# A two-block transformer kernel on one core: its SBUF tiles allocated from both ends, with other start addresses

## The reference, cut to what matters

```python
# first block, DEPTH = 2 layers
h = rms_norm(x, attn_norm_g[l])
pa, pb, pc = split_sizes(h @ w_in[l], (A_PROJ, B_PROJ, C_PROJ))
ya, yb, yc = rwkv7_mixer(pa, ...), dilated_mixer(pb, ...), mla_mixer(pc, ...)
x = x + jnp.concatenate([ya, yb, yc], axis=-1) @ w_out[l]
h = rms_norm(x, ffn_norm_g[l])
x = x + (jax.nn.silu(h @ ffn_w_gate[l]) * (h @ ffn_w_up[l])) @ ffn_w_down[l]   # D_FF = 2816
# second block, DEPTH = 2 layers
#   h @ w_in_2 (IN_COLS = 3584), stick-breaking, MoBA and memory attention, gates,
#   x = x + mixed @ w_out_2, then a last rms_norm
```

## The kernel before, in words

| tile | start | modulo 1024 | minus w_hi, modulo 1024 |
|---|---|---|---|
| w_hi (and w_lo, w_raw) | 58560 | 192 | 0 |
| act_hi, act_lo | 24704, 32896 | 128 | -64 |
| mixed_hi, mixed_lo | 106240, 114432 | 768 | -448 |
| gated_hi, gated_lo, layer 0 | 131328, 153856 | 256 | +64 |
| gated_hi, gated_lo, layer 1 | 131424, 153952 | 352 | +160 |
| mem_hi, mem_lo | 131424, 139616 | 352 | +160 |

## Time and profile before

### The profile page before, as it was taken

The page is one execution under the profiler, slowest core; times in us unless marked ns, Lnnn a source line. Parts: engine busy times, 40 slices in busy tenths (PEclk is TensorE's granted clock), DMA queues, the critical chain, the costliest instruction groups (busy, mean ns, idle before and its releaser), DMA issues.

```text
span 967.2 us, 20420 instructions
## 1 busy us (share of the span) xinstructions
PE 937.9 (97%) x8862; PEld 886.4 (92%) x8862; DVE 680.7 (70%) x972; ACT 554.6 (57%) x851; POOL 7.6 (1%) x12
## 2 busy tenths in 40 slices
PE   8899999999999999999999999999999999999996
PEld 7788799999999988878999999998899899999896
DVE  6898666866744679966776666348699677698674
ACT  6873466645443578355654444337487666486565
POOL 0000000000000001000000000000000000000000
PEclk9999999999999999999999999999999999999999
DMA  9341115565555433211466654554353335453241
GB/s 337 159 165 55 46 58 194 205 228 210 180 194 198 175 128 135 89 46 46 155 218 229 242 189 174 185 199 140 131 175 131 94 137 189 149 174 135 94 141 69
DMA packets 23145, 149.89 MB, mean 155 GB/s; under 512 B 2576, under 2 KB 2832, under 8 KB 6032
## 3 DMA queue, kind: packets, MB, share of 16 engines
q1 hardware_dynamic: 23056, 148.59, 43.2%
HBM read 147.26 MB, written 1.05 MB: 153 GB/s over the span
## 4 chain that ended last, share of the span: by engine, by line
PE 68%; DVE 18%; ACT 9%; issue 2%; DMA 1%; SPq 0%; DVEq 0%; ACTq 0%
PE bank L1889 8%; PE bank L1890 8%; PE bank L1891 8%; DVE w_lo L275 6%; PE bank L2109 4%; PE bank L1912 4%; PE bank L1911 4%; PE bank L1913 4%; ACT w_hi L269 3%; PE bank L2110 3%; PE bank L2111 3%; PE bank L2114 2%; PE bank L2116 2%; PE bank L2115 2%; ACT act_hi L372 1%
## 5 line engine op out<-in xcount | busy, mean ns | idle before, releaser
L275 DVE TENSOR_TENSOR w_lo<-w_raw,w_hi 128x1024 fp32r<-128x1024 f32 x256 | 306.4, 1225 | 108.5 <-ACT w_hi L269 107.6
L269 ACT ACTIVATE w_hi<-w_raw 128x1024 fp32r<-128x1024 f32 x256 | 259.5, 1053 | 209.0 <-PE bank L1891 103.3
L1889 PE MATMUL bank<-act_hi,w_hi 128*128 128x256 f32 x704 | 196.7, 279 | 1.6 <-DVE w_lo L275 1.0
L1890 PE MATMUL bank<-act_lo,w_hi 128*128 128x256 f32 x704 | 195.9, 278 | 0.0
L1891 PE MATMUL bank<-act_hi,w_lo 128*128 128x256 f32 x704 | 195.9, 278 | 0.0
L1889 PEld LDWEIGHTS bank<-act_hi,w_hi 128*128 128x128 f32 x704 | 133.5, 190 | 2.4 <-issue 1.4
L1890 PEld LDWEIGHTS bank<-act_lo,w_hi 128*128 128x128 f32 x704 | 132.2, 188 | 0.1
L1891 PEld LDWEIGHTS bank<-act_hi,w_lo 128*128 128x128 f32 x704 | 132.1, 188 | 0.0
L2109 PE MATMUL bank<-act_hi,w_hi 128*128 128x256 f32 x352 | 100.7, 286 | 3.9 <-DVE w_lo L275 2.4
L1912 PE MATMUL bank<-gated_lo,w_hi 128*128 128x256 f32 x352 | 98.7, 280 | 0.0
L1911 PE MATMUL bank<-gated_hi,w_hi 128*128 128x256 f32 x352 | 98.5, 280 | 0.0
(11 more groups left out here) (370 smaller groups left out, 1994.7 us busy)
## 6 DMA issues: line engine op xcount, KB each, us to landing
w_raw<-in_w_ffn SPq DMA_DIRECT2D x66, 1024.0 KB, 4.8
w_raw<-in_w_mix SPq DMA_DIRECT2D x62, 1024.0 KB, 4.9
small_w<-in_small SPq DMA_DIRECT2D x2, 1280.0 KB, 7.5
w_raw<-in_w_mix SPq DMA_DIRECT2D x8, 256.0 KB, 6.0
x_res<-in_x_channels SPq DMA_DIRECT2D x4, 256.0 KB, 5.6
probs<-in_w_mix SPq DMA_DIRECT2D x2, 512.0 KB, 7.5
probsT<-in_w_mix SPq DMA_DIRECT2D x1, 1024.0 KB, 10.2
mem<-in_mem_channels SPq DMA_DIRECT2D x1, 1024.0 KB, 7.4
```

The lines of the kernel that those rows point to most:

```text
L269: self.nc.scalar.activation(hi, self.piece(self.raw_slot(g), p), ACT.Copy).then_inc(self.hi_ready, 1)
L275: self.nc.vector.tensor_tensor(lo, self.piece(self.raw_slot(g), p), hi.bitcast(fp32), ALU.subtract).then_inc(self.lo_ready, 1)
L1889: TE.matmul(o, hi[:, w], HI[:, k, :], start=(k == 0 and x == 0), stop=False)
L1890: TE.matmul(o, hi[:, w], LO[:, k, :], start=False, stop=False)
```

## The change

Tiles can now be allocated from the upper end downwards (`top=True`). The weight stream's three tiles, the squares, norms, constants, parameters and tables go to the upper end; the activation pairs and the stages' own tiles stay at the lower end. Four unused tiles are added: `between` (128 bytes) above the weights, `below_mixed` (32 bytes), `below_gated` (96 bytes, in layer 1 alone) and `below_mem` (64 bytes). No instruction, size, order or semaphore is changed; only start addresses are.

```diff
+BETWEEN = 32
...
-        raw = K.sb("w_raw", [P, 2, CHUNK])
-        hi, lo = K.sb("w_hi", [P, 2, CHUNK], f32r), K.sb("w_lo", [P, 2, CHUNK], f32r)
+        raw = K.sb("w_raw", [P, 2, CHUNK], top=True)
+        hi, lo = (K.sb(f"w_{x}", [P, 2, CHUNK], f32r, top=True) for x in ("hi", "lo"))
...
-        self.PRMS = self.sb("prm", [P, WIDTH["prm"] + N_PRMS])
+        self.PRMS = self.sb("prm", [P, WIDTH["prm"] + N_PRMS], top=True)
+        self.RSALL = self.sb("norm_rs", [P, T + NT], top=True)
+        self.cst_sb = {"both": self.sb("consts_both", [P, WIDTH["both"]], top=True), "prm": self.PRMS}
+        self.sb("between", [P, BETWEEN], top=True)
         self.st = Stream(self)
...
-        return (c or self.ctx).enter_context(self.nc.sbuf_tensor(name, shape, dt))
+        return (c or self.ctx).enter_context(
+            self.nc.sbuf_tensor(name, shape, dt, side="right" if top else "left"))
...
+    if layer:
+        K.sb("below_gated", [P, 24], c=c)
     GHI = K.sb("gated_hi", [P, FK, T], f32r, c)
...
+    K.sb("below_mem", [P, 16], c=c)
     MHI = K.sb("mem_hi", [P, KT, T], f32r, c)
...
-            first["rope_tables"] = K.sb("rope_tables", [P, 4, T], c=c)
-            first["positions"] = K.sb("positions", [P, T], i32, c)[:, :]
+            K.sb("below_mixed", [P, 8], c=c)
+            first["rope_tables"] = K.sb("rope_tables", [P, 4, T], c=c, top=True)
+            first["positions"] = K.sb("positions", [P, T], i32, c=c, top=True)[:, :]
...
-            second["mem"] = K.sb("mem", [P, KT, T], c=c)[:, :, :]
-            second["gates"] = K.sb("gates", [P, 8, T], c=c)
+            second["mem"] = K.sb("mem", [P, KT, T], c=c, top=True)[:, :, :]
+            second["gates"] = K.sb("gates", [P, 8, T], c=c, top=True)
```

More of the change, by code:

```diff
@@ L302, in __init__, with sb @@
         self.LO = self.sb("act_lo", [P, KT, T], f32r)
-        self.PRMS = self.sb("prm", [P, WIDTH["prm"] + N_PRMS])
+        self.PRMS = self.sb("prm", [P, WIDTH["prm"] + N_PRMS], top=True)
+        self.RSALL = self.sb("norm_rs", [P, T + NT], top=True)
+        self.cst_sb = {"both": self.sb("consts_both", [P, WIDTH["both"]], top=True), "prm": self.PRMS}
+        self.sb("between", [P, BETWEEN], top=True)
         self.st = Stream(self)
-        self.SQ = self.sb("squares", [P, 3, 512])
-        self.RSALL = self.sb("norm_rs", [P, T + NT])
+        self.SQ = self.sb("squares", [P, 3, 512], top=True)
         self.RSB, self.RS = self.RSALL[:, 0:T], self.RSALL[:, T:T + NT]
-        self.cst_sb = {"both": self.sb("consts_both", [P, WIDTH["both"]]), "prm": self.PRMS}
         self.PS = ctx.enter_context(nc.psum_tensor("bank", [P, 8 * 512], fp32))
         self.banks = [self.PS[:, 512 * i:512 * (i + 1)] for i in range(8)]
-    def sb(self, name, shape, dt=fp32, c=None):
+    def sb(self, name, shape, dt=fp32, c=None, top=False):
         self.named[name] = self.named.get(name, -1) + 1
         name = f"{name}_{self.named[name]}" if c else name
-        return (c or self.ctx).enter_context(self.nc.sbuf_tensor(name, shape, dt))
+        return (c or self.ctx).enter_context(
+            self.nc.sbuf_tensor(name, shape, dt, side="right" if top else "left"))
     def sem(self, name):
@@ L2789, in program @@
         K = Kernel(nc, ctx, io)
-        GAINS = K.sb("gains", [P, KT])
+        GAINS = K.sb("gains", [P, KT], top=True)
         block = ctx.enter_context(nc.Block())
@@ L2800, in program @@
             K.sb("small_w_end", [P, N_SMALL + 4 * T - 2 * KT * T], c=c)
-            K.cst_sb["first"] = K.sb("consts_first", [P, WIDTH["first"]], c=c)
+            K.cst_sb["first"] = K.sb("consts_first", [P, WIDTH["first"]], c=c, top=True)
             stage_start(K, block, norm, GAINS[:, :], first)
@@ L2815, in program @@
         with ExitStack() as c:
-            K.cst_sb["second"] = K.sb("consts_second", [P, WIDTH["second"]], c=c)
-            second["mem"] = K.sb("mem", [P, KT, T], c=c)[:, :, :]
-            second["gates"] = K.sb("gates", [P, 8, T], c=c)
+            K.cst_sb["second"] = K.sb("consts_second", [P, WIDTH["second"]], c=c, top=True)
+            second["mem"] = K.sb("mem", [P, KT, T], c=c, top=True)[:, :, :]
+            second["gates"] = K.sb("gates", [P, 8, T], c=c, top=True)
             second["mem_tokens"] = second["gates"].rearrange("p (t x) c -> p t (x c)", t=NT)
[L2820 to L2824, removed]
+            second["mem_rs_row"] = K.sb("mem_rs_row", [P, T], c=c, top=True)
+            second["mem_ss"] = K.sb("mem_ss", [P, NT], c=c, top=True)
+            second["mem_rs"] = K.sb("mem_rs", [P, NT], c=c, top=True)
+            SQ2 = K.sb("scaled_squares", [P, 3, 512], c=c, top=True)
+            R1 = K.sb("first_rs", [P, T + NT], c=c, top=True)
             chunk = DEPTH * (N_MIX1 + N_FFN)
```

## The result

The changed kernel takes **978.57 us** (median of 7 runs, 978.04 to 979.57) beside 973.11 us (968.36 to 974.66, 7 runs) for the kernel before in the same job: 1.0071 times as long, 95% interval 1.0052 to 1.0090. It is slower by 0.7%. The forecast was 970.5 us. The likeliest case was wrong; rival A, to which I gave a chance of 0.2, named 978.6 us.

The account below looks back on a forecast made before the run. TensorE was taken as the bound, matmul count times pitch. Terms of -1.3, -0.2, +0.2 and +0.3 summed to -1.0 us on a level of 971.5, giving 970.5 us; 8-in-10 range 961 to 979 us.

Parts of the forecast that it names:

- rival A: Act matmuls: the distance to the weights decides whether the fast rhythm exists, -128 lacks it; 978.6 us, chance 0.2.
- What bounds the kernel: TensorE, busy 97% of the span: time is mainly the number of matmuls times their start-to-start distance, the pitch.
- Act, 3936 matmuls: Matmuls moving the act pair: still multiples of 64, same fast and slow rhythms, 0; bounds -6.7 to +10.6 us.
- My argument against A: Act's distance: +64 modulo 128 equals -64, and role-exchanged products were partly fast at another distance; no size given.
- Mem and weights over mem: 480 matmuls moving mem, from 118.0 to 115.2 ns, -1.3 us; 96 with mem stationary, 120.0 to 117.8, -0.2 us.
- Gated of layer 0 and mixed: 912 matmuls leaving the multiples of 64, from 117.8 to 118.0 ns: +0.2 us, bounds -0.5 to +0.8, -3.9 if fast.
- Gated of layer 1: 528 matmuls staying 32 off a multiple of 64: 0; bounds -0.7 to 0, or -2.7 us if fast.
- Weights over act: 384 matmuls with weights moving and act stationary: pitch 0.8 ns longer, +0.3 us; bounds about -0.8 to +1.8.
- ScalarE, VectorE, DMA at 0: Work outside TensorE: same operation lengths at either address class, taken as 0, +-1 us.
- Rival B: All moving pairs: small negative distances are always fast; 961.3 us, or 952 if all pairs are fast; chance 0.2.
- Rival C: Whole kernel: addresses play no part, weight-tile order and PSUM halves make the differences; 971.5 us, chance 0.1.
- The level: Starting time for the forecast: rhythm drawn anew in each execution, so the mean of four executions, 971.5 us.

Follow-up runs that it names:

- e1: Kernel before with 64 unused bytes below the weight tiles, so only act's distance to stationary weights changes, -64 to -128: 979.58 us, 1.0086 times the kernel before.
- e5: Changed kernel with act put back to distance -64, other pairs' distances kept modulo 256: 969.46 us, 1.0033 times the kernel before.
- e10: Kernel before with only 128 unused bytes added between w_hi and w_lo: 963.21 us, 0.9965 times the kernel before.
- e4: Separate program, only rows of 36 matmuls, sweeping the moving pair's distance to the weights, 0 to 992 bytes by 32: pitches 113.3 to 120.3 ns.
- e6: Separate program, only rows of 36 matmuls, distances 0 to 248 bytes in steps of 8: no row under 113.3 ns.
- e2: Changed kernel with weights 64 bytes lower and three spacers removed, every moving pair at -64: 971.38 us, 0.9997 times the kernel before.
- e9: Changed kernel with every moving pair at -64 and 128 unused bytes between w_hi and w_lo: 960.28 us, 0.9938 times the kernel before.

## Why the prediction was wrong

- **What bounds the kernel: right.** Time is matmuls times pitch, and only the pitch moved.
- **The step that failed: "Act, 3936 matmuls. Same class as before (both multiples of 64), so the same two rhythms: 0."** The class is the distance modulo 256, not a shared multiple of 64. The sweep shows that my one class held four different ones, with 120.0, mostly 117.8, 118.7, and 113.3 or 117.8 ns; -128 is the third and has no fast row in 24; e1 shows the same in the kernel. In the changed kernel the term is 3936 x (118.7 - 115.3) = 13.4 us of PE time, beyond my bound of +10.6, whose slow end was before's own slow rhythm. The trace of before held no row at -128, and I priced it by a class that no row had tested.
- **Rival A, its mechanism: right** (e1 alone brings 1.0086; e5 takes it back, wholly by the pitch, half by its ratio). **Its number, 978.6, was right partly by luck, since two errors cancel:** it took 117.9 for act where 118.7 came, 3.1 us too little, and counted all of it on the path where part was covered. PE's pitches sum to 13.4 for act, +0.7 for weights over act, +0.2 mixed, -0.4 gated, -0.9 mem, -0.2 weights over mem = +12.8 us, and the span grew by 10.6. The rest was covered by other work, by the windows mostly in the first block's two mixers: there PE's busy time grew by 2.7 and 1.3 us and the stages by 1.3 and 0.2, while the feed-forwards' projections grew by 6.3 of 7.0 us. My argument against A, that +64 modulo 128 is the same as -64, took a period of 128 where it is 256; at +64 5 rows of 24 are fast.
- **Mem and weights over mem:** the direction was right (116.1 for the 115.2 I took; 117.8). **Gated of layer 0 and mixed:** 117.3 and 118.5, inside the bounds. **Gated of layer 1:** 118.3, inside. **Weights over act:** +1.9 ns where I took +0.8.
- **ScalarE, VectorE, DMA at 0: right,** within 0.3 us of busy time. The rule of the Trainium skill that I set against the rows (SBUF — State Buffer, "Who interferes with whom": TensorE's two ports wait for nobody) would have given no change; in e1 64 unused bytes cost 10 us, so here the measurement decides against it, if "waits for nobody" is read as "at one speed".
- **Rival B, negative distances always fast: refuted.** -128 is never fast, -96 and -32 are not either. Its price for an always fast act, 961.3 us, is close to what e10 (963.21) got by another means, and by luck, since mixed and gated of layer 0 are fast there as well. **Rival C, addresses play no part: refuted** by e1.
- **The level:** that the rhythm is drawn anew in each execution fits before's runs, most of which lie at some 965, 969 and 973 us, though only one was traced. The steps ceased where the fast rhythm doesn't exist: the changed kernel's 7 runs are within 1.5 us, so its slow rhythm was no longer a draw.

## What to carry to other kernels

Where TensorE is the bound and the matmuls run without a gap, list the start addresses of each moving and stationary tile and look at their distance modulo 256 bytes: with 128 x 256 fp32r matmuls a change of 64 bytes was worth 10 us in 970. If two equal blocks of one trace have two pitches, the median hides a draw; find a layout that takes the draw away (here +-64 with 128 bytes more between the high and low weights, 0.62% under before) ahead of tuning the rest. A class of addresses read from a trace holds only for the distances that stand in it; for a new one, run a row of matmuls by itself first.

## What the hardware showed that I had not expected

- The commonest pitches are discrete. At the full granted clock of 2.4 GHz, 113.33 ns are 272 cycles, 120.0 are 288, and the means 117.78, 118.67 and 117.33 are 848 cycles in 3 matmuls, 1424 in 5 and 1408 in 5: each of these totals is a multiple of 16 cycles (6.67 ns). In the start times of before's trace the fast act rows keep one phase of a 6.67 ns raster, within 1.4 ns, throughout the execution, and the rows at 117.78 step through three. Which rhythm a row takes goes with the phase of its start only in part: in e4 at distance 192, one stretch of 4 ns of the raster holds the starts of all 16 fast rows, but of 4 of the 8 slow ones too. That the phase explains the draw is a guess; I ran nothing that sets it, and what in the chip makes the raster is not shown.
- One distance off a multiple of 64, 112 bytes, was at 113.3 in all 6 rows of e6, more regular than 64 (1 of 6) or 192 (4 of 6). Whether it would be so in the kernel wasn't tried.
- A distance that is good for one role is not for the other: with 128 bytes between the splits the products with the weights stationary and act moving gained 2.5 ns and those with the weights moving lost 3.6 (e2 against e9).
